# Which engine forms the low parts of the feed-forward weights: GpSimd before, VectorE after

## The chip, the cores and the metric

The kernel runs on one core of a Trainium2 chip. A core has five engines that each run their own instruction queue in order: TensorE (PE in the profile, with its weight loads as PEld), VectorE (DVE), ScalarE (ACT), GpSimd (POOL) and SyncE (SP), which here issues DMA transfers. The engines meet only at semaphores. The metric is device time in microseconds of one launch. Before the change three runs took 1326.4 to 1327.08 us, with a median of 1326.59.

## The reference

Two decoder layers on 512 tokens of width 1024 in fp32. Each layer is a mixer (gated linear attention and mLSTM in layer 0, stick-breaking and dilated attention in layer 1) and a SwiGLU feed-forward part, each with a modulation of its input and output that comes from a conditioning vector, and a normalization behind it. What the change touches is the feed-forward part, whose hidden width D_FF is 2816:

```
for layer in range(DEPTH):
    mod = c_act @ ada_w[layer] + ada_b[layer]            # six rows of 1024: shift, scale, gate, twice
    ...
    x = layer_norm(RES_ALPHA * x + (1.0 + g_m) * y, ln_g[layer, 0], ln_b[layer, 0])
    hf = x * (1.0 + sc_f) + sh_f
    yf = (jax.nn.silu(hf @ ffn_w1[layer]) * (hf @ ffn_w3[layer])) @ ffn_w2[layer]
    x = layer_norm(RES_ALPHA * x + (1.0 + g_f) * yf, ln_g[layer, 1], ln_b[layer, 1])
```

## The kernel before

**Split products.** TensorE multiplies fp32 operands as two parts. A weight tile arrives from HBM in `raw`; ScalarE writes its high part to `w_hi` (`to_hi`, L903), and another engine writes the low part, `w_lo = raw - w_hi`. The activations are split in the same way into `h_hi` and `h_lo`. A product is then three matmuls: weight high by activation low, high by high, and low by high (L1391 to L1393 in gate and up, L1441 to L1443 in down). A weight slot is 128 x 1024 values, 512 KB, and `raw`, `w_hi` and `w_lo` are rings of four slots each. Semaphores count the slots: `w_hi_ready`, `w_lo_ready`, and `slot_done` when TensorE has used one.

**Gate and up** (`ffn` on each engine). D_FF is cut into 11 steps of two 128-column blocks. A step uses four slots, two of gate and two of up, 96 matmuls. GpSimd forms the low parts of all of them (`split_range`, L832), one after another in a loop of four. VectorE's `step` (L2668) then does two things: `combine_weights` (L2660 to L2666) forms sums and differences of down-weight blocks, and L2677 to L2687 multiply gate by up into `hid` and form four sums of `hid`. Both kinds of sums serve the down product, which uses Strassen's scheme in Winograd's form: seven products of half-size blocks instead of eight. The down weights of a step are loaded into `combos` by DMAs that ScalarE issues, combined in place, and stored to a scratch area in HBM, 1 MB each way; ScalarE waits for `combo_step` before it issues the store.

**Modulation.** In layer 0 the loop of gate and up also computes the modulation rows of what follows. `two_steps` (L2710) runs two steps of the loop, and ahead of each it does four modulation products: `ada_acc` gets a 128 x 1024 tile of `ada_w` times one column of `c_act` added (L2717; L2720 for the first of eight). The tiles come through `ada_raw`, two buffers. Layer 1 has at most one smaller group of modulation products a step (`ada_block`), whose tiles are loaded apart.

**SyncE's loads.** In the loop of layer 0, SyncE issues in turn a weight load and a modulation load (L764 to L771):

```
for u in range(4):
    sp.wait_ge(sem("w_lo_ready"), 4 * j + (s0 + u - RAW + 1))
    sp.dma_start(raw[:, (s0 + u) % RAW, :], wstream[...])
    sp.wait_ge(sem("ada_step"), 4 * j + (36 + u - 1))
    sp.dma_start(ada_raw[:, u % 2, :], astream[...])
```

A weight load waits for the split four slots earlier, and a modulation load for the product that used its buffer; a waiting load holds back those behind it. The loads of iteration j begin at the stage's slot 4j, and its modulation waits count the products of step j. In layer 1 weight loads wait for the split four slots earlier alone.

**Down.** It has 42 slots, in the order P1, P5 and P6 in turn (18 slots), then P2, P3, P7 and P4 with six each; five pairs and a single one make the 11 steps. Some slots are 128 x 512, the rest 128 x 1024. Two slots of P4 (`HELD`) go to space that `hid_r` has left. GpSimd forms the low parts of the first four slots (`LO_FROM`) and from slot 30 on (`LO_TO`, L853 to L870), and VectorE those between (`down`, L2742, `lo`). Beside the weights, the factors of the products are split: ScalarE does the high parts (`a_hi`, `b1_hi`, `b2_hi`) and VectorE the low ones (`a_lo`, `b1_lo`, `b2_lo` at L2761 and L2762). In the last part, VectorE's and ScalarE's `b2` parts of step k stand behind the split of slot 21 + k.

**The end of down.** When P3's slots are used, the upper two token blocks are complete. VectorE's `norm` forms the residual and its statistics (`residual`, L2528 to L2546) and ScalarE normalizes (`normalizer`, L1133 to L1149), while TensorE works on P7 and P4, whose weights ScalarE still has to split. The place of `normalize(0)` among the `hi` calls of `down` is fixed in the code.

Of the kernel before, what the change touches and what calls it, by code (L numbers as in the profile page):

```python
# [17 lines left out]
ALU = mybir.AluOpType  # L18
# [21 lines left out]
RING = 4  # L40
# [68 lines left out]

DOWN = down_slots()  # L110
N_DOWN = len(DOWN)
LO_FROM, LO_TO = 4, 30
HELD = 38


# [115 lines left out]
def build_program(nc, wstream, astream, xT, vecs, const, const0, wa_up, dsel, rel, ln_rows, out):  # L231
# [595 lines left out]
    @block.gpsimd  # L827
    def _(pool):
        def split(s, slot):

            pool.wait_ge(sem("w_hi_ready"), s + 1)
            nc.gpsimd.tensor_tensor(w_lo[:, slot, :], raw[:, slot % RAW, :], w_hi[:, slot, :].bitcast(F32),  # L832
                                    ALU.subtract).then_inc(sem("w_lo_ready"), 1)

        assert RAW == RING

        def split_range(a, b):
            if b - a < 2 * RING:
                for s in range(a, b):
                    split(s, s % RING)  # L840
                return
            up, down = -(-a // RING) * RING, b // RING * RING
            for s in range(a, up):
                split(s, s % RING)
            with pool.Fori(up // RING, down // RING) as i:
                for u in range(RING):
                    split(RING * i + u, u)
            for s in range(down, b):
                split(s, s % RING)

        pool.wait_ge(sem("w_lo_ready"), len(FIRST))
        at_ = len(FIRST)
        for x in sorted(list(extra) + [DOWN0, DOWN1]):  # L853
            split_range(at_, x)
            at_ = x + 1
            if x in extra:
                pool.wait_ge(sem("w_hi_ready"), x + 1)
                nc.gpsimd.tensor_tensor(extra[x][1], raw[:, x % RAW, :], extra[x][0].bitcast(F32), ALU.subtract
                                        ).then_inc(sem("w_lo_ready"), 1)
                continue  # L860
            for s in range(x, x + LO_FROM):
                split(s, s % RING)
            pool.wait_ge(sem("w_lo_ready"), x + LO_TO)
            for m in range(LO_TO, N_DOWN):
                pool.wait_ge(sem("w_hi_ready"), x + m + 1)
                down_lo(nc.gpsimd, x, m).then_inc(sem("w_lo_ready"), 1)
            at_ = x + N_DOWN
        pool.wait_ge(sem("in_rows"), 16)
        for tb in range(1, TB - 1):
            pool.wait_ge(sem("xh_ready"), TB * 3 + tb + 1)  # L870
            nc.gpsimd.tensor_tensor(x_rows(tb), x_rows(tb), by_chunk(rows_gb[:, 0, :]), ALU.mult).then_inc(sem("scaled"), 1)
            pool.wait_ge(sem("scaled"), tb)
            nc.gpsimd.tensor_tensor(x_rows(tb), x_rows(tb), by_chunk(rows_gb[:, 1, :]), ALU.add).then_inc(sem("out_ready"), 1)
# [3 lines left out]
    def _(act):  # L877
# [41 lines left out]
        def warm_sqrt():  # L919

            nc.scalar.activation(warm[:], eps_col, ACT.Sqrt)
# [261 lines left out]
        def down(layer):  # L1183
# [4 lines left out]
            def hi(m):  # L1188
                to_hi(d + m, (d + m) % RING)
# [25 lines left out]
            for g in range(6):  # L1215
# [11 lines left out]
                    i.then_inc(sem("p1_copied"), 1)  # L1227
                hi(3 * g + 4)
                hi(3 * g + 5)
            for k in range(HALF_K):  # L1230
                hi(21 + k)
                b2_hi(k)
            hi(32)
            hi(33)
            warm_sqrt()
            normalize(0)
            hi(34)
            hi(35)
            normalize(1)
            for m in range(36, N_DOWN):  # L1240
                hi(m)
            done[0] = d + N_DOWN
            if layer == 1:
# [873 lines left out]
    def _(dve):  # L2117
# [528 lines left out]
        def ffn(layer, rest):  # L2646
# [18 lines left out]
                dve.wait_ge(sem("combo_step"), before + 3)  # L2665
                V.tensor_tensor(b21, b21, b11, ALU.subtract).then_inc(sem("combo_step"), 1)  # L2666

            def step(j, between=None):  # L2668

                combine_weights(j)  # L2670
                if between:
                    between()
                for b in range(2):
                    dve.wait_ge(*((sem("bank_full"), 2 * j + f0) if b == 0 else (sem("slot_done"), 4 * j + (s0 + 4))))
                    dve.wait_ge(sem("silu_ready"), 2 * j + (FC * layer + 1 + b))
                    split = lambda ap: ap.rearrange("q (o a x) -> q o a x", o=1, x=256)
                    V.tensor_tensor(block(j, (slice(0, 5, 4), slice(3, 7, 3))[b]), split(tmp[:, b, :]), split(ps[:, up + b, :]), ALU.mult  # L2677
                                    ).then_inc(sem("prod_ready"), 1)
                a11, s1, s2, a12, a21, s3, a22 = (block(j, a) for a in range(7))
                before = 4 * j + 4 * HALF_K * layer  # L2680
                dve.wait_ge(sem("prod_ready"), 2 * j + (FC * layer + 2))
                V.tensor_tensor(s1, a21, a22, ALU.add).then_inc(sem("s_step"), 1)
                V.tensor_tensor(s3, a11, a21, ALU.subtract).then_inc(sem("s_step"), 1)
                dve.wait_ge(sem("s_step"), before + 2)
                V.tensor_tensor(s2, s1, a11, ALU.subtract).then_inc(sem("s_step"), 1)  # L2685
                dve.wait_ge(sem("s_step"), before + 3)
                V.tensor_tensor(a21, a12, s2, ALU.subtract).then_inc(sem("s_step"), 1)  # L2687
# [21 lines left out]

            def two_steps(it, between=None):  # L2710

                for u in range(2):
                    for k in range(4 * u, 4 * u + 4):
                        dve.wait_ge(sem(f"ada_landed{k % 2}"), 64 * it + 16 * (12 + k // 2 + 1))
                        if k:
                            dve.wait_ge(sem("ada_step"), 8 * it + (40 + k))
                            V.scalar_tensor_tensor(ada_acc[:], ada_raw[:, k % 2, :], c_act[:, k:k + 1], ada_acc[:], ALU.mult,  # L2717
                                                   ALU.add).then_inc(sem("ada_step"), 1)
                        else:
                            V.tensor_scalar(ada_acc[:], ada_raw[:, 0, :], c_act[:, 0:1], None, ALU.mult  # L2720
                                            ).then_inc(sem("ada_step"), 1)
                    if u:
                        dve.wait_ge(sem("ada_step"), 8 * it + 48)
                        fold_rows()
                    step(2 * it + (u + 1), between if u else None)

            with dve.Fori(0, FC // 4 - 1) as it:
                two_steps(it)
# [12 lines left out]
        def down(layer):  # L2741
# [3 lines left out]
            def lo(m):  # L2745

                dve.wait_ge(sem("w_hi_ready"), d + m + 1)
                if m == LO_FROM:
                    dve.wait_ge(sem("w_lo_ready"), d + m)
                down_lo(V, d, m).then_inc(sem("w_lo_ready"), 1)  # L2750

            def b1_lo(k):
# [10 lines left out]
                                ALU.subtract).then_inc(sem("x_ready"), 1)  # L2763

            for g in range(6):
                if 3 * g + 3 >= LO_FROM:
                    lo(3 * g + 3)
                for k in (2 * g + 2, 2 * g + 3):
                    if k < HALF_K:
                        a_lo(layer, k)  # L2770
# [13 lines left out]
                        ins = V.tensor_tensor(u2_kept(r), p1_kept(r), by_half(ps[:, 5 + 2 * r, :]), ALU.add)  # L2784
                    ins.then_inc(sem("kept_added"), 1)
                lo(3 * g + 5)
            for k in range(HALF_K):
                if 21 + k < LO_TO:
                    lo(21 + k)
                b2_lo(k)  # L2790

        ffn(0, norm(0, "out0"))
        gate_col(1)
# [225 lines left out]
```

## Time and profile before

| | before |
|---|---|
| median of three runs | 1326.59 us (1326.4 to 1327.08) |
| the profiled execution | 1326.98 us, of which the span is 1325.2 |
| TensorE busy | 1254.8 us (95%) |
| TensorE weight loads busy | 1038.9 us (78%) |
| VectorE busy | 901.2 us (68%) |
| ScalarE busy | 528.5 us (40%) |
| GpSimd busy | 476.5 us (36%) |

The span is from the first to the last instruction of the profiled execution. Busy time is summed over instructions and says nothing of when they ran. The gate and up stage of layer 0 lies at about 319 to 547 us of the span, its down stage at 556 to about 665; layer 1's gate and up stage lies at about 965 to 1205 us and its down stage follows until the end. A timeline row begins with the start and the duration of an instruction or of a few equal ones in a row (xN), and ends with the idle time ahead of it on its engine and what ended that.

### The profile page before, as it was taken

The page shows a single profiled execution, that of the slowest core. Times are in us where ns is not written, and L with a number is a line of the kernel's source. Part 1 is how long each engine was busy: PE and PEld are TensorE (multiplying, and loading weights), DVE is VectorE, ACT ScalarE, POOL GpSimd, SP SyncE. Part 2 cuts the span into 40 slices and gives each one's busy share as a digit, 9 for nine tenths or more (in the row PEclk, how much of TensorE's full clock was granted, in tenths as well). Part 3 has the DMA queues.
Part 4 walks back from the last instruction along what each step waited for, and adds up shares of the span by engine and source line. Part 5 has one row for each costly group of instructions (what it writes and reads, how often), then busy time and mean ns, then how long its engine had stood idle before and what let it go on. Part 6 is the DMA issues. An engine that isn't in the chain of part 4 may idle for free.

```text
span 1325.2 us, 17193 instructions
## 1 busy us (share of the span) xinstructions
PE 1254.8 (95%) x6298; PEld 1038.9 (78%) x6298; DVE 901.2 (68%) x1244; ACT 528.5 (40%) x767; POOL 476.5 (36%) x195
## 2 busy tenths in 40 slices
PE   7999999998999999599899999999999999999996
PEld 6878887787787778488687777888888888888874
DVE  5489768868778777667766633358697636447785
ACT  3443364542212122366552455527342222225653
POOL 0243332423444444300645332222245444442046
PEclk9999999999999999799999999999999999999998
DMA  9981654534687777557446542212156665645843
GB/s 333 188 175 65 222 160 128 190 112 165 248 286 275 264 281 270 189 152 236 129 164 230 159 124 92 64 63 75 39 176 251 226 233 203 214 173 162 245 151 116
DMA packets 129362, 239.51 MB, mean 181 GB/s; under 512 B 18523, under 2 KB 83307, under 8 KB 126356
## 3 DMA queue, kind: packets, MB, share of 16 engines
q1 hardware_dynamic: 110792, 188.07, 45.5%
q10 hardware_dynamic: 18508, 50.62, 10.5%
q8 instruction: 38, 0.62, 0.2%
q14 instruction: 24, 0.20, 0.0%
HBM read 212.11 MB, written 27.59 MB: 181 GB/s over the span
## 4 chain that ended last, share of the span: by engine, by line
PE 60%; issue 17%; POOL 9%; DVE 8%; DMA 3%; ACT 1%; POOLq 0%; SPq 0%; DVEq 0%; ACTq 0%
PE ps L1391 10%; PE ps L1393 10%; PE ps L1392 10%; POOL w_lo L832 8%; PE ps L1441 4%; PE ps L1442 4%; PE ps L1443 4%; DMA ada_raw<-astream 2%; PE ps L1590 2%; PE ps L1591 2%; PE ps L1592 2%; PE ps L1556 1%; PE ps L1558 1%; PE ps L1557 1%; PE ps L1943 1%
## 5 line engine op out<-in xcount | busy, mean ns | idle before, releaser
L832 POOL TENSOR_TENSOR w_lo<-raw,w_hi 128x1024 fp32r<-128x1024 f32 x157 | 397.7, 2542 | 655.1 <-ACT w_hi L903 654.9
L903 ACT ACTIVATE w_hi<-raw 128x1024 fp32r<-128x1024 f32 (+1 forms) x235 | 238.9, 1031 | 498.2 <-DMA raw<-wstream 181.6
L1391 PE MATMUL ps<-h_lo,w_hi 128*128 128x512 f32 (+2 forms) x1064 | 399.5, 375 | 15.9 <-POOL w_lo L832 13.9
L1393 PE MATMUL ps<-h_hi,w_lo 128*128 128x512 f32 (+2 forms) x1064 | 394.6, 371 | 0.0
L1392 PE MATMUL ps<-h_hi,w_hi 128*128 128x512 f32 (+2 forms) x1064 | 394.6, 371 | 0.0
L1391 PEld LDWEIGHTS ps<-h_lo,w_hi 128*128 128x128 f32 (+1 forms) x1064 | 200.9, 189 | 57.3 <-issue 20.0
L1393 PEld LDWEIGHTS ps<-h_hi,w_lo 128*128 128x128 f32 (+1 forms) x1064 | 200.7, 189 | 34.8
L1392 PEld LDWEIGHTS ps<-h_hi,w_hi 128*128 128x128 f32 (+1 forms) x1064 | 200.9, 189 | 33.2
L650 POOL TENSOR_TENSOR w_lo<-raw,w_hi 128x1024 fp32r<-128x1024 f32 (+1 forms) x20 | 44.6, 2250 | 160.0 <-ACT w_hi L903 159.8
L2717 DVE SCALAR_TENSOR_TENSOR ada_acc<-ada_raw,c_act,ada_acc 128x1024 f32<-128x1024 f32 x35 | 58.8, 1679 | 45.1 <-DMA ada_raw<-astream 44.6
L2677 DVE TENSOR_TENSOR hid<-tmp,ps 128x512 f32<-128x512 f32 (+1 forms) x44 | 29.1, 683 | 86.2 <-PE ps L1393 86.2
L650 DVE TENSOR_TENSOR w_lo<-raw,w_hi 128x1024 fp32r<-128x1024 f32 (+1 forms) x52 | 57.6, 1121 | 30.8 <-ACT w_hi L903 30.4
L1441 PE MATMUL ps<-w_hi,hid_r 128*128 128x512 f32 x160 | 63.9, 400 | 8.2 <-issue 7.6
L2148 DVE SCALAR_TENSOR_TENSOR ada_acc<-ada_raw,c_act,ada_acc 128x1024 f32<-128x1024 f32 x35 | 60.8, 1737 | 12.0 <-DMA ada_raw<-astream 10.1
L1441 PE MATMUL ps<-w_hi,a_hl 128*128 128x512 f32 x132 | 52.5, 398 | 14.4 <-DVE mod L2154 14.4
L1442 PE MATMUL ps<-w_hi,hid_r 128*128 128x512 f32 x160 | 63.6, 398 | 0.0
L1443 PE MATMUL ps<-w_lo,hid_r 128*128 128x512 f32 x160 | 63.6, 398 | 0.0
L1442 PE MATMUL ps<-w_hi,a_hl 128*128 128x512 f32 x132 | 52.2, 395 | 0.0
L1443 PE MATMUL ps<-w_lo,a_hl 128*128 128x512 f32 x132 | 52.1, 394 | 0.0
L2685 DVE TENSOR_TENSOR hid<-hid 128x256 f32<-128x256 f32 (+1 forms) x22 | 48.1, 2186 | 1.6
L1441 PEld LDWEIGHTS ps<-w_hi,hid_r 128*128 128x128 f32 x160 | 30.8, 193 | 16.7 <-issue 9.3
L1590 PE MATMUL ps<-w_hi,h_lo 128*128 128x512 f32 (+1 forms) x112 | 41.8, 373 | 0.7 <-DVE kc L2807 0.7
(318 smaller groups left out, 2033.5 us busy)
## 6 DMA issues: line engine op xcount, KB each, us to landing
raw<-wstream SPq DMA_DIRECT2D x161, 512.0 KB, 4.5
ada_raw<-astream SPq DMA_DIRECT2D x80, 512.0 KB, 4.5
combos<-wstream ACTq DMA_DIRECT2D x22, 1024.0 KB, 5.5
combo_scratch<-combos ACTq DMA_DIRECT2D x22, 1024.0 KB, 3.9
raw<-combo_scratch SPq DMA_DIRECT2D x88, 256.0 KB, 3.3
raw<-wstream SPq DMA_DIRECT2D x66, 256.0 KB, 3.8
ada_first<-astream SPq DMA_DIRECT2D x16, 256.0 KB, 6.7
ada_first<-astream SPq DMA_DIRECT2D x8, 512.0 KB, 10.5
```

Source lines behind the costliest of these rows:

```text
L650: return engine.tensor_tensor(w_lo[:, s % RING, 0:n], raw[:, s % RAW, 0:n], w_hi[:, s % RING, 0:n].bitcast(F32), ALU.subtract)
L832: nc.gpsimd.tensor_tensor(w_lo[:, slot, :], raw[:, slot % RAW, :], w_hi[:, slot, :].bitcast(F32), ALU.subtract).then_inc(sem("w_lo_ready"), 1)
L903: nc.scalar.activation(w_hi[:, slot, 0:n], raw[:, slot, 0:n], ACT.Copy).then_inc(sem("w_hi_ready"), 1)
L1391: pe.matmul(o, w_h, x_l, start=start, stop=False)
L1392: pe.matmul(o, w_h, x_h, start=False, stop=False)
L1393: return pe.matmul(o, w_l, x_h, start=False, stop=stop)
L1441: pe.matmul(o, x_lo, w_h, start=begin, stop=False, skip_group_check=True)
L1442: pe.matmul(o, x_hi, w_h, start=False, stop=False, skip_group_check=True)
L1443: return pe.matmul(o, x_hi, w_l, start=False, stop=end, skip_group_check=True)
L1590: pe.matmul(o, h_lo[:, k, tokens], w_hi[:, s % RING, w], start=start, stop=False)
L2148: V.scalar_tensor_tensor(ada_acc[:], src, c_act[:, k:k + 1], ada_acc[:], ALU.mult, ALU.add).then_inc(sem("ada_step"), 1)
L2717: V.scalar_tensor_tensor(ada_acc[:], ada_raw[:, k % 2, :], c_act[:, k:k + 1], ada_acc[:], ALU.mult, ALU.add).then_inc(sem("ada_step"), 1)
```

## The change

VectorE takes over the low parts that GpSimd formed in both feed-forward stages: in gate and up all slots but the first four of a stage, in down the first thirty-two, so that GpSimd keeps the last ten, which belong to the products P7 (its last four) and P4. In layer 0, the four modulation products of a step are cut in two pairs, and the four splits too: two behind each pair. The slots that a step splits are the running step's fourth and the next step's first three. In down the `b2` parts come two steps at a time, so that they end by slot 26, and ScalarE does one more slot ahead of `normalize(0)`. TensorE's and SyncE's instructions are those of before.

```
-LO_FROM, LO_TO = 4, 30
+LO_TO = 32
...
-            split_range(at_, x)
+            split_range(at_, x if x in extra else SLOTS["ffn0" if x == DOWN0 else "ffn1"][0] + RING)
...
-            for s in range(x, x + LO_FROM):
-                split(s, s % RING)
...
-            for k in range(HALF_K):
-                hi(21 + k)
-                b2_hi(k)
-            hi(32)
-            hi(33)
+            for n in range(6):
+                hi(21 + n)
+                for k in (2 * n, 2 * n + 1):
+                    if k < HALF_K:
+                        b2_hi(k)
+            for m in range(27, 34):
+                hi(m)
             warm_sqrt()
+            hi(34)
             normalize(0)
-            hi(34)
             hi(35)
+            hi(36)
             normalize(1)
-            for m in range(36, N_DOWN):
+            for m in range(37, N_DOWN):
                 hi(m)
...
-            def step(j, between=None):
-
+            def step_lo(j, u):
+
+                slot = (s0 + u) % RING
+                dve.wait_ge(sem("w_hi_ready"), 4 * j + (s0 + u + 1))
+                V.tensor_tensor(w_lo[:, slot, :], raw[:, slot, :], w_hi[:, slot, :].bitcast(F32), ALU.subtract
+                                ).then_inc(sem("w_lo_ready"), 1)
+
+            def step(j, between=None, beside=None):
+
+                if beside:
+                    beside(0)
+                if not isinstance(j, int) or j:
+                    step_lo(j, 3)
+                else:
+                    dve.wait_ge(sem("w_lo_ready"), s0 + RING)
+                step_lo(j, 4)
                 combine_weights(j)
+                if beside:
+                    beside(1)
+                step_lo(j, 5)
+                step_lo(j, 6)
                 if between:
                     between()
...
-                for u in range(2):
-                    for k in range(4 * u, 4 * u + 4):
+                def ada(u, part):
+
+                    for k in range(4 * u + 2 * part, 4 * u + 2 * part + 2):
...
-                    if u:
+                    if u and part:
                         dve.wait_ge(sem("ada_step"), 8 * it + 48)
                         fold_rows()
-                    step(2 * it + (u + 1), between if u else None)
+
+                for u in range(2):
+                    step(2 * it + (u + 1), between if u else None, lambda part: ada(u, part))
...
             def lo(m):
 
                 dve.wait_ge(sem("w_hi_ready"), d + m + 1)
-                if m == LO_FROM:
-                    dve.wait_ge(sem("w_lo_ready"), d + m)
                 down_lo(V, d, m).then_inc(sem("w_lo_ready"), 1)
...
             for g in range(6):
-                if 3 * g + 3 >= LO_FROM:
-                    lo(3 * g + 3)
+                lo(3 * g + 3)
...
-            for k in range(HALF_K):
-                if 21 + k < LO_TO:
-                    lo(21 + k)
-                b2_lo(k)
+            for n in range(6):
+                lo(21 + n)
+                for k in (2 * n, 2 * n + 1):
+                    if k < HALF_K:
+                        b2_lo(k)
+            for m in range(27, LO_TO):
+                lo(m)
```

The first place is VectorE's program at the head of the first two steps inside layer 0's loop. Before, it reads so (ISA and REGISTER_ALU rows are waits and the counts for them; `combos` rows are `combine_weights`):

```order
L2720 TENSOR_SCALAR ada_acc<-ada_raw,c_act 128x1024
L2716 ISA
L2717 SCALAR_TENSOR_TENSOR ada_acc<-ada_raw,c_act,ada_acc 128x1024
L2714 REGISTER_ALU
L2716 REGISTER_ALU
L2717 SCALAR_TENSOR_TENSOR ada_acc<-ada_raw,c_act,ada_acc 128x1024
L2716 REGISTER_ALU
L2717 SCALAR_TENSOR_TENSOR ada_acc<-ada_raw,c_act,ada_acc 128x1024
L2659 ISA
L2660 TENSOR_TENSOR combos<-combos 128x2x256
L2661 ISA
L2662 TENSOR_TENSOR combos<-combos 128x2x256
```

The same place of VectorE's program after the change, up to the combination:

```order
L2740 TENSOR_SCALAR ada_acc<-ada_raw,c_act 128x1024
L2736 ISA
L2737 SCALAR_TENSOR_TENSOR ada_acc<-ada_raw,c_act,ada_acc 128x1024
L2672 ISA
L2673 TENSOR_TENSOR w_lo<-raw,w_hi 128x1024
L2672 REGISTER_ALU
L2673 TENSOR_TENSOR w_lo<-raw,w_hi 128x1024
L2660 ISA
L2661 TENSOR_TENSOR combos<-combos 128x2x256
```

And from the end of the combination on, ahead of the gate by up product:

```order
L2667 TENSOR_TENSOR combos<-combos 128x2x256
L2734 REGISTER_ALU
L2736 REGISTER_ALU
L2737 SCALAR_TENSOR_TENSOR ada_acc<-ada_raw,c_act,ada_acc 128x1024
L2736 REGISTER_ALU
L2737 SCALAR_TENSOR_TENSOR ada_acc<-ada_raw,c_act,ada_acc 128x1024
L2672 REGISTER_ALU
L2673 TENSOR_TENSOR w_lo<-raw,w_hi 128x1024
L2672 REGISTER_ALU
L2673 TENSOR_TENSOR w_lo<-raw,w_hi 128x1024
```

The four modulation products stood together ahead of the combination; now two stand ahead of it and two behind it, and each pair is followed by two splits that wait for ScalarE's high parts.

The second place is ScalarE's program at the end of layer 0's down stage, around `normalize(0)` (`cols`, `nmr` and `xa` rows). Before:

```order
L903 ACTIVATE w_hi<-raw 128x1024
L1209 ACTIVATE hid_r<-hid 128x256
L1210 ACTIVATE hid_r<-hid 128x256
L903 ACTIVATE w_hi<-raw 128x1024 x2
L921 ACT_TABLE_LOAD
L921 ACTIVATE warm<-vec_eps 128x1
L1133 ACTIVATE cols<-mv,vec_eps 128x1
L1134 ACTIVATE cols<-mv 128x1
L1146 ACTIVATE nmr<-cols,cst,rstd 128x1
L1149 ACTIVATE xa<-xa,nmr,rstd 128x8x128
L903 ACTIVATE w_hi<-raw 128x1024
L903 ACTIVATE w_hi<-raw 128x512
```

The same place after the change:

```order
L901 ACTIVATE w_hi<-raw 128x512
L901 ACTIVATE w_hi<-raw 128x1024 x4
L919 ACT_TABLE_LOAD
L919 ACTIVATE warm<-vec_eps 128x1
L901 ACTIVATE w_hi<-raw 128x1024
L1131 ACTIVATE cols<-mv,vec_eps 128x1
L1132 ACTIVATE cols<-mv 128x1
L1144 ACTIVATE nmr<-cols,cst,rstd 128x1
L1147 ACTIVATE xa<-xa,nmr,rstd 128x8x128
L901 ACTIVATE w_hi<-raw 128x512
L901 ACTIVATE w_hi<-raw 128x1024
```

One weight slot more is ahead of the wait for the statistics, and the `b2` parts (`hid_r<-hid`) have moved forward.

The third place is VectorE's program at the end of the same stage, ahead of the residual (`ps` rows; `scl` rows derive the next modulation). Before:

```order
L650 TENSOR_TENSOR w_lo<-raw,w_hi 128x512
L2761 TENSOR_TENSOR hid_r<-hid,hid_r 128x256
L2762 TENSOR_TENSOR hid_r<-hid,hid_r 128x256
L2761 TENSOR_TENSOR hid_r<-hid,hid_r 128x256
L2762 TENSOR_TENSOR hid_r<-hid,hid_r 128x256
L2761 TENSOR_TENSOR hid_r<-hid,hid_r 128x256
L2762 TENSOR_TENSOR hid_r<-hid,hid_r 128x256
L2182 SCALAR_TENSOR_TENSOR scl<-mod,vec 128x8
```

After the change:

```order
L2781 TENSOR_TENSOR hid_r<-hid,hid_r 128x256
L2782 TENSOR_TENSOR hid_r<-hid,hid_r 128x256
L650 TENSOR_TENSOR w_lo<-raw,w_hi 128x1024 x2
L650 TENSOR_TENSOR w_lo<-raw,w_hi 128x512
L650 TENSOR_TENSOR w_lo<-raw,w_hi 128x1024 x2
L2183 SCALAR_TENSOR_TENSOR scl<-mod,vec 128x8
```

The last `b2` parts stood directly ahead of the residual; now five weight splits stand there.

## Rows read from the trace of the kernel before

**Rows 1.** The page: busy time of each engine; costliest groups, and by shape.

```profile
PE 1254.8 (95%) x6298; PEld 1038.9 (78%) x6298; DVE 901.2 (68%) x1244; ACT 528.5 (40%) x767; POOL 476.5 (36%) x195
...
L832 POOL TENSOR_TENSOR w_lo<-raw,w_hi 128x1024 fp32r<-128x1024 f32 x157 | 397.7, 2542 | 655.1 <-ACT w_hi L903 654.9
...
L650 DVE TENSOR_TENSOR w_lo<-raw,w_hi 128x1024 fp32r<-128x1024 f32 x42 | 51.0, 1224 | 28.8 <-ACT w_hi L903 28.4
```

**Rows 2.** Windows: length, busy of PE, PEld, DVE, ACT, POOL, granted clock, DMA share, GB/s.

```profile
328.30:332.20 3.90, 3.90 (x9) 3.08 (x10) 3.87 (x3) 1.74 (x3) 2.88 (x1) 0.50 0.85 307
376.00:398.00 22.00, 21.69 (x96) 17.64 (x94) 17.04 (x15) 4.78 (x6) 9.77 (x4) 1.00 0.77 270
556.40:560.90 4.50, 4.50 (x11) 3.53 (x12) 2.81 (x4) 0.00 (x0) 0.00 (x0) 0.50 0.00 0
649.70:653.10 3.40, 3.40 (x10) 2.66 (x9) 0.00 (x0) 3.24 (x4) 1.78 (x2) 0.50 0.74 233
970.00:1202.00 232.00, 232.00 (x1088) 194.20 (x1086) 133.56 (x136) 63.01 (x73) 109.23 (x43) 1.00 0.59 211
1291.40:1294.80 3.40, 3.40 (x10) 2.63 (x9) 2.63 (x2) 3.40 (x4) 1.79 (x2) 0.50 0.86 273
```

**Rows 3.** Timeline of VectorE over one step of layer 0's loop.

```profile
358.94 1.28 DVE L2677 TENSOR_TENSOR hid<-tmp,ps 128x512 f32 x2
360.49 0.43 DVE L2682 TENSOR_TENSOR hid<-hid  x1 [0.27 <-DVE hid L2677]
...
363.82 2.51 DVE L2687 TENSOR_TENSOR hid<-hid  x1
...
366.32 0.74 DVE L2720 TENSOR_SCALAR ada_acc<-ada_raw,c_act 128x1024 f32<-128x1024 f32 x1
...
370.42 1.28 DVE L2717 SCALAR_TENSOR_TENSOR ada_acc<-ada_raw,c_act,ada_acc 128x1024 f32<-128x1024 f32 x1 [2.03 <-DMA ada_raw<-astream]
...
376.54 0.68 DVE L2660 TENSOR_TENSOR combos<-combos 128x512 f32<-128x512 f32 x1
```

**Rows 4.** Timeline of SyncE's DMA queue in the same step.

```profile
367.09 0.33 SPq L770 DMA_DIRECT2D ada_raw<-astream  x1
367.62 0.33 SPq L767 DMA_DIRECT2D raw<-wstream  x1
...
369.29 0.33 SPq L767 DMA_DIRECT2D raw<-wstream  x1
```

**Rows 5.** Timeline of ScalarE in the same step.

```profile
372.00 1.06 ACT L903 ACTIVATE w_hi<-raw 128x1024 fp32r<-128x1024 f32 x1 [10.27 <-DMA raw<-wstream]
375.67 1.06 ACT L903 ACTIVATE w_hi<-raw 128x1024 fp32r<-128x1024 f32 x1 [2.61 <-DMA raw<-wstream]
```

**Rows 6.** VectorE's first modulation product of step 1 and of step 10.

```profile
318.93 0.75 DVE L2720 TENSOR_SCALAR ada_acc<-ada_raw,c_act 128x1024 f32<-128x1024 f32 x1
...
526.12 2.66 DVE L2717 SCALAR_TENSOR_TENSOR ada_acc<-ada_raw,c_act,ada_acc 128x1024 f32<-128x1024 f32 x2
```

**Rows 7.** TensorE's waits in layer 0: step 1, one later step, down's start.

```profile
328.27 0.77 PE L1391 MATMUL ps<-h_lo,w_hi 128*128 128x512 f32 x1 [5.67 <-POOL w_lo L832]
...
398.52 0.47 PE L1391 MATMUL ps<-h_lo,w_hi 128*128 128x512 f32 x1 [0.83 <-POOL w_lo L832]
...
556.38 0.77 PE L1441 MATMUL ps<-w_hi,a_hl 128*128 128x512 f32 x1 [14.22 <-DVE mod L2154]
```

**Rows 8.** The end of down: layer 0 (VectorE, ScalarE, TensorE), then layer 1.

```profile
633.65 2.62 DVE L2762 TENSOR_TENSOR hid_r<-hid,hid_r 128x256 fp32r<-128x256 f32 x1
...
643.68 0.30 ACT L1133 ACTIVATE cols<-mv,vec_eps 128x1 f32<-128x1 f32 x1 [7.33 <-DVE mv L2539]
...
645.77 1.56 ACT L903 ACTIVATE w_hi<-raw 128x1024 fp32r<-128x1024 f32 x2
...
649.33 0.47 PE L1441 MATMUL ps<-w_hi,hid_r 128*128 128x512 f32 x1 [4.79 <-issue]
...
1290.58 0.47 PE L1441 MATMUL ps<-w_hi,hid_r 128*128 128x512 f32 x1 [2.12 <-issue]
```

## The prediction

> **What bounds the kernel now.** I read the page first, then the windows by stage, then one step of the first layer's gate and up loop engine by engine, then the waits around its end and around the end of both down stages. The page shows TensorE busy 95% of the span and VectorE 68% [rows 1]; the shares hide that stages differ. In the windows the second layer's loop has TensorE busy 232.00 of 232.00 us, while a quiet stretch of the first layer's loop takes 22.0 us for one step of 96 matmuls [rows 2]. So in the second layer nothing but the matmuls sets the pace, and splits moved there can gain nothing.
>
> In the first layer a step is longer than its matmuls. The first modulation product of step 1 ends at 318.93 + 0.75 = 319.68 and that of step 10 at 526.12 + 1.28 = 527.40 [rows 6]: nine steps take 207.7 us, 23.1 each, 1.1 more than the matmuls. The missing time is TensorE waiting for a split: 5.67 us in step 1, then about a microsecond a step (0.83 in the row shown), and 14.22 us before the down stage [rows 7]. What it waits for can be followed in one step. VectorE ends its first modulation product at 366.32 + 0.74 = 367.06 [rows 3]; SyncE, which was waiting for exactly that, issues the next modulation load at 367.09 and only behind it, at 367.62, the weight load of the fourth slot of the running step; the next weight load goes out at 369.29, after the second product [rows 4]. ScalarE starts on the two weights at 372.00 and 375.67 [rows 5]. The weight stream of this layer is thus paced by VectorE's modulation products, two products per two slots. Before the change VectorE does all four products before anything else of the step, and no VectorE instruction waits for a weight; GpSimd does.
>
> **The change part by part.** Per layer 46 splits go from GpSimd (2542 ns each) to VectorE (1224 ns) [rows 1]: 40 of gate and up, the first four of down, and down's 31st and 32nd. GpSimd's 110 us were beside other work; VectorE's 56 us a layer stand in an in-order queue, and that is what has to be priced.
>
> First layer, gate and up. VectorE's step becomes: products 1 and 2, split of the fourth slot, split of the next step's first, combination of down weights, products 3 and 4, splits of the next step's second and third, gate times up, four sums. SyncE's program is unchanged. So the two weights whose splits stand right behind products 1 and 2 are those that SyncE issues after products 1 and 2, and the same again with 3 and 4: VectorE now sits through the landing of each pair, twice a step, and queued behind the waiting split are the combination, the other products, and with them the next weight loads. I call L the time from the end of an odd product to the moment ScalarE can start on the pair's second weight. From below: issued 2.23 us after the product (369.29 - 367.06), landing as fast as the weight that had one transfer ahead of it, 372.00 - 367.62 = 4.38: L = 6.6. From above, as that row has it: 375.67 - 367.06 = 8.6 [rows 4, 5]. I take 7.5, the middle: the same four loads in the same order, but without the next four on their heels, and in the second pair with a 1 MB store beside them. The serial rest of a step: high part 1.06 and split 1.22 with hand-offs, 2.5, twice, 5.0; combination 4 x 0.68 with gaps 2.9; product 3, 1.3; gate times up 1.3; four sums of 0.43, 1.75; modulation and next product 1 (0.74 or 1.28) 1.1 [rows 1, 3, 5]. Together 13.35, so a step is 13.35 + 2L: 28.4 us, with 26.6 and 30.6 as ends. Against 23.1 that is +5.3 a step (+3.5 to +7.5), over the nine steps +47.7 (+31.5 to +67.5).
>
> What is taken off in that loop: the sums and combinations no longer wait for GpSimd; the last sum took 2.51 us against 0.43 for one that did not wait [rows 3]. That relief is already in the terms above. At the loop's start I count -1 (between -2 and 0: two waits on GpSimd go, three splits come). Behind the last step 556.38 - 527.40 = 29.0 us pass before down's first matmul [rows 6, 7]; the combined weights are now stored while products 3, 4 and the splits run instead of ahead of the split pairs, but the pair's wait is added: -2.5 (between -5 and 0).
>
> The Trainium skill, page "SBUF — State Buffer", section "Who interferes with whom", says that a VectorE instruction with two SBUF inputs and a GpSimd instruction that reads SBUF exclude each other for a whole instruction; the 2.51 us row agrees. By that rule alone every step would lose about 4 us of waiting and none would be added: the second rival's mechanism. Against the change speaks the page "DMA: Bandwidth & Descriptors", section "Anatomy of one DMA": a semaphore wait happens on the issuing sequencer, before a transfer is dispatched. The 0.03 us between product and issue agree. By it a weight behind a waiting load is not even under way, and the pair's landing comes on top.
>
> TensorE in this loop: two waits of 2 to 3 us a step. The trace shows it at 0.50 of its clock (1.2 of 2.4 GHz) for some microseconds after its waits of 5.67, 14.22, 4.79 and 2.12 us [rows 2, 7, 8]. One stretch of 3.4 us costs 1.7; two a step make 22.0 + 3.4 = 25.4, still under 28.4, so I cost it at nothing; without that cover it would be the first rival.
>
> Second layer, gate and up: 0. Its weight loads wait only for the split four slots earlier, so each is under way a step ahead; VectorE's 133.56 us of 232 [rows 2] plus 49 for 40 splits leaves room. From below 0, since TensorE never waits there; from above +10, a microsecond a step.
>
> Down, both layers. Before, VectorE's last pair splits run against GpSimd's (2.62 us for one subtraction, as long as the sum of 2.51 [rows 3, 8]), so the first residual and ScalarE's normalization are late. ScalarE waits 7.33 us for them with the next weight behind it in its queue, starts on that at 645.77, and TensorE stands 4.79 us [rows 8], then runs 3.4 us at half clock [rows 2], 1.7 more. After the change the pair splits end by slot 26, VectorE does slots 30 and 31 itself, and ScalarE takes the 35th slot before it waits: I expect the stall gone, -6.5. The second layer's is 2.12 and again 1.7 [rows 2, 8]: -3.8. Together -10.3, between -11 and 0. New in this part: two pair splits per slot, 1.22 + 2 x 0.86 = 2.9 us of VectorE for 2.7 of TensorE over six slots, covered by the slots already split.
>
> Sum: 47.7 - 1 - 2.5 - 10.3 = +34. The profiled execution took 1326.98 (span 1325.2 and 1.8 around it), 0.4 above the median of the runs: 1361 against it, 1360 as a median. Ends: 31.5 - 7 - 11 = +13, 1340; 67.5 and no relief but down's, 1384.
>
> **The rivals.** First, the half clock: if the two waits a step kept TensorE at 1.2 GHz throughout, 96 matmuls would take about 43 us instead of 22, and nine steps 180 more: 1500. For it: every wait above 2 us in the rows was followed by a half-clock stretch. Against: full clock came back within 4 to 5 us of work each time. Second, the other side: the waits for landings are covered and only the relief counts. Then the loop falls to TensorE's 22.0 (9 x 1.1 = 10), step 1's 5.67 goes, and down gives 10: 1301. It decides where 13.35 + 2L reaches 23.1, L = 4.9; for it the 2.51 us rows, against it that the pair's second load is issued 2.2 us in and a transfer with one ahead of it already needs 4.4. Third, the down stages stay as they are, because the residual or the last splits on GpSimd find another wait: +44, 1371. Fourth, the pair lands much nearer to its issue than any row (L 5 to 6): 1327 to 1340.
>
> **How the numbers follow.** Forecast 0.70; half clock 0.05; other side 0.09; no gain in down 0.12; fourth 0.04, of which three parts in four too small to tell. 0.2% is about what a measurement of this kernel can tell from no change. Slower 0.70 + 0.05 + 0.12 + 0.01 = 0.88, same 0.03, faster 0.09. The range leaves out the half clock, the other side and the fourth, and is the forecast's own: 1338 to 1384.
>
> **What would show it.** Right: in the first layer's loop VectorE idle twice a step with ScalarE's high part as releaser, some 4 us each, steps of 26.6 to 30.6 us, TensorE waiting twice a step for VectorE's split; the second layer's loop still without a TensorE wait; no wait of 4.79 and 2.12 late in down. Wrong: first-layer steps of 22 us, waits for a weight in the second layer, or those late waits still there.

## The result and the profile after

The changed kernel takes 1378.94 us (median of four runs, 1378.49 to 1382.55) against 1326.84 before: ratio 1.0399, 95% interval 1.0381 to 1.0417. The forecast was 1360 with 1338 to 1384 as its range; direction and mechanism held, and a loss of 34 us was forecast where 52 came. The profiled execution took 1379.32 us with a span of 1377.4, 52.2 more than before.

The page after the change, first the busy times, then the group of VectorE's new splits (busy us, mean ns of one, idle time ahead of it and what ended that):

```profile
PE 1269.4 (92%) x6298; PEld 1049.3 (76%) x6298; DVE 873.1 (63%) x1336; ACT 529.3 (38%) x767; POOL 243.6 (18%) x103
...
L2673 DVE TENSOR_TENSOR w_lo<-raw,w_hi 128x1024 fp32r<-128x1024 f32 x86 | 104.7, 1223 | 211.5 <-ACT w_hi L901 211.5
```

VectorE took over 105 us of splits in gate and up and yet is busy 28 us less than before [rows 1], since its other instructions no longer meet GpSimd's: the sum of `hid` that took 2.51 us in [rows 3] takes 0.42 after the change. But it now stands 211.5 us ahead of these splits, waiting for ScalarE's high part. Where that happens is told by the first modulation product of step 1 and of step 10 (as [rows 6]):

```profile
318.28 0.75 DVE L2740 TENSOR_SCALAR ada_acc<-ada_raw,c_act 128x1024 f32<-128x1024 f32 x1
...
595.00 2.66 DVE L2737 SCALAR_TENSOR_TENSOR ada_acc<-ada_raw,c_act,ada_acc 128x1024 f32<-128x1024 f32 x2
```

Nine steps take 596.28 - 319.03 = 277.25 us, 30.8 each instead of 23.1: +69.5 us. The chain of waits over one step shows what a step is made of (start, us, what):

```profile
443.54 1.29 DVE ada_acc L2737
444.85 0.33 SPq L770
...
445.73 6.03 DMA raw<-wstream
451.86 1.07 ACT w_hi L901
...
454.10 0.69 DVE combos L2661
...
456.88 1.29 DVE ada_acc L2737
458.33 0.33 SPq L770
...
458.85 1.04 SPq L767
459.98 1.14 SPq L770
461.32 6.08 DMA raw<-wstream
467.42 1.07 ACT w_hi L901
...
469.65 1.29 DVE hid L2696 x2
...
472.90 1.29 DVE ada_acc L2737
```

TensorE is not in it at all. Twice a step the chain goes from a product to SyncE, from there into a weight load of 6 us, to ScalarE and back to VectorE. In the windows (columns as in [rows 2]: the last 1.9 us of the wait in step 2 with the half-clock stretch behind it, the step above, layer 1's loop) TensorE is busy 25.05 of 30.8 us in layer 0's step, at half clock for a part of it, and 232.00 of 232.00 us in layer 1:

```profile
342.00:348.60 6.60, 4.69 (x11) 3.76 (x12) 4.41 (x6) 1.56 (x2) 0.00 (x0) 0.50 0.55 205
...
443.50:474.30 30.80, 25.05 (x96) 19.82 (x95) 15.43 (x20) 5.20 (x6) 0.00 (x0) 0.89 0.57 204
...
1027.00:1259.00 232.00, 232.00 (x1087) 194.29 (x1087) 137.33 (x182) 63.01 (x73) 0.00 (x0) 1.00 0.59 212
```

TensorE's waits in step 1, in step 2 and, in two pieces around eight small matmuls of the modulation, ahead of down, which answer to [rows 7]; then ScalarE ahead of the normalization in down (7.33 us of idle in [rows 8]):

```profile
326.22 0.47 PE L1392 MATMUL ps<-h_lo,w_hi 128*128 128x512 f32 x1 [2.97 <-DVE w_lo L2673]
...
343.91 0.77 PE L1392 MATMUL ps<-h_lo,w_hi 128*128 128x512 f32 x1 [6.56 <-DVE w_lo L2673]
...
614.78 0.30 PE L1605 MATMUL ps<-ada_part,cst 128*32 128x8 f32 x8 [5.33 <-DVE ada_part L2159]
...
621.95 0.76 PE L1442 MATMUL ps<-w_hi,a_hl 128*128 128x512 f32 x1 [6.86 <-DVE mod L2155]
```

```profile
702.79 0.29 ACT L1131 ACTIVATE cols<-mv,vec_eps 128x1 f32<-128x1 f32 x1 [0.40 <-DVE mv L2540]
```

ScalarE waits 0.40 us there, and between 690 and 724 us no TensorE row shows a wait. From the start of the first to the start of the last matmul layer 0's down takes 107.9 us (116.1 before, from 556.38 to 672.5 us of the span, where the section on time and profile has about 665) and layer 1's 105.0 (110.1). So the 52 us are +69.5 in layer 0's loop, -13.4 in the two down stages, and -4 at the loop's two ends.

### The profile page after: what moved, and what is told of

It is laid out like the page before. It is cut to its first block, busy times and chain, and to the rows that moved or that the text cites. A ratio compares the mean times of both kernels' runs of the same rounds, so it can differ in the third digit from the quotient of the medians.

```text
span 1377.4 us, 17095 instructions
## 1 busy us (share of the span) xinstructions
PE 1269.4 (92%) x6298; PEld 1049.3 (76%) x6298; DVE 873.1 (63%) x1336; ACT 529.3 (38%) x767; POOL 243.6 (18%) x103
## 4 chain that ended last, share of the span: by engine, by line
PE 60%; DVE 16%; DMA 10%; issue 6%; ACT 3%; SPq 2%; POOL 2%; DVEq 0%; POOLq 0%; ACTq 0%
PE ps L1392 9%; PE ps L1393 9%; PE ps L1394 9%; DMA raw<-wstream 8%; PE ps L1442 4%; PE ps L1444 4%; PE ps L1443 4%; DVE ada_acc L2737 3%; ACT w_hi L901 2%; PE ps L1591 2%; PE ps L1844 2%; PE ps L1846 2%; PE ps L1845 2%; PE ps L1593 2%; PE ps L1592 2%
## 5 line engine op out<-in xcount | busy, mean ns | idle before, releaser
L1392 PE MATMUL ps<-h_lo,w_hi 128*128 128x512 f32 (+2 forms) x1064 | 407.7, 383 | 48.6 <-DVE w_lo L2673 43.0
L1393 PE MATMUL ps<-h_hi,w_hi 128*128 128x512 f32 (+2 forms) x1064 | 402.1, 378 | 0.0
L1394 PE MATMUL ps<-h_hi,w_lo 128*128 128x512 f32 (+2 forms) x1064 | 401.4, 377 | 0.0
L832 POOL TENSOR_TENSOR w_lo<-raw,w_hi 128x1024 fp32r<-128x1024 f32 x69 | 174.6, 2539 | 364.2 <-ACT w_hi L901 364.1
L2673 DVE TENSOR_TENSOR w_lo<-raw,w_hi 128x1024 fp32r<-128x1024 f32 x86 | 104.7, 1223 | 211.5 <-ACT w_hi L901 211.5
L1393 PEld LDWEIGHTS ps<-h_hi,w_hi 128*128 128x128 f32 (+1 forms) x1064 | 205.5, 193 | 34.5
L650 POOL TENSOR_TENSOR w_lo<-raw,w_hi 128x1024 fp32r<-128x1024 f32 (+1 forms) x16 | 33.8, 2137 | 735.5 <-ACT w_hi L901 735.5
L650 DVE TENSOR_TENSOR w_lo<-raw,w_hi 128x1024 fp32r<-128x1024 f32 (+1 forms) x58 | 65.0, 1128 | 34.4 <-ACT w_hi L901 33.7
L2149 DVE SCALAR_TENSOR_TENSOR ada_acc<-ada_raw,c_act,ada_acc 128x1024 f32<-128x1024 f32 x35 | 61.2, 1749 | 11.8 <-DMA ada_raw<-astream 9.7
L1442 PE MATMUL ps<-w_hi,a_hl 128*128 128x512 f32 x132 | 52.2, 395 | 6.9 <-DVE mod L2155 6.9
L2737 DVE SCALAR_TENSOR_TENSOR ada_acc<-ada_raw,c_act,ada_acc 128x1024 f32<-128x1024 f32 x35 | 44.9, 1281 | 1.3 <-DVE ada_acc L2740 0.5
L1593 PE MATMUL ps<-w_lo,h_hi 128*128 128x512 f32 (+1 forms) x112 | 40.4, 361 | 0.0
```

What stands on the lines that cost most here:

```text
L650: return engine.tensor_tensor(w_lo[:, s % RING, 0:n], raw[:, s % RAW, 0:n], w_hi[:, s % RING, 0:n].bitcast(F32), ALU.subtract)
L1392: pe.matmul(o, w_h, x_l, start=start, stop=False)
L1393: pe.matmul(o, w_h, x_h, start=False, stop=False)
L1394: return pe.matmul(o, w_l, x_h, start=False, stop=stop)
L1442: pe.matmul(o, x_lo, w_h, start=begin, stop=False, skip_group_check=True)
L2673: V.tensor_tensor(w_lo[:, slot, :], raw[:, slot, :], w_hi[:, slot, :].bitcast(F32), ALU.subtract).then_inc(sem("w_lo_ready"), 1)
```

## The experiments

The theory under test: VectorE sits through the landing of weights that SyncE issues only behind VectorE's own modulation products, and a step is a serial rest plus the two waits L. Each ratio is against the kernel before, run beside that experiment, whose median was 1327.82, 1327.61 or 1328.25 us; differences between two experiments are of their medians.

**Weight loads three slots earlier in SyncE's program.**

```
-        for s in range(s0, s0 + 4):
+        AHEAD = 3
+        for s in range(s0, s0 + 4 + AHEAD):
             load(s)
-        with sp.Fori(1, FC // 2) as j:
+        with sp.Fori(1, FC // 2 - 1) as j:
             for u in range(4):
-                sp.wait_ge(sem("w_lo_ready"), 4 * j + (s0 + u - RAW + 1))
+                w = s0 + u + AHEAD
+                sp.wait_ge(sem("w_lo_ready"), 4 * j + (w - RAW + 1))
...
+        for u in range(4):
+            if u < 4 - AHEAD:
+                load(s0 + 4 * (FC // 2 - 1) + u + AHEAD)
+            load_ada(4 * (FC // 2 - 1) + 36 + u)
```

> The changed kernel, with one thing moved: in SyncE's loop of layer 0 each weight load is issued three slots earlier among the modulation loads, so that the weights that VectorE splits in a step are under way before that step's modulation products. Theory (VectorE sits through the landing of weights that are issued only behind its own products): the two waits a step go, a step falls from 30.8 us to TensorE's 22 to 23, nine steps give back 70 to 79 us: 1300 to 1309. Rival 1 (the 49 us of splits in VectorE's in-order queue are themselves the cost): VectorE's work in a step is what it was, the time stays above 1360. Rival 2 (the transfers are slow because loads and the 1 MB stores share the DMA engines, wherever they are issued): steps of 26 to 29 us, 1335 to 1362.

1290.62 us, ratio 0.9712 (0.9696 to 0.9728): 88 us less than the change alone, and 37 less than before. The window over layer 0's loop, and TensorE's wait ahead of down:

```profile
320.00:526.00 206.00, 206.00 (x935) 169.45 (x933) 149.75 (x180) 50.58 (x56) 0.00 (x0) 1.00 0.81 293
```

```profile
533.36 0.77 PE L1448 MATMUL ps<-w_hi,a_hl 128*128 128x512 f32 x1 [6.91 <-DVE mod L2161]
```

TensorE is busy for the whole 206 us at full clock. VectorE does exactly the work of the changed kernel, so the work is not the cost (rival 1), and the same loads and stores run beside them (rival 2). It went below the range that I gave: the steps run at 22 us, as expected, and the waits in steps 1 and 2, which I had not counted apart, went too.

**Small modulation loads.**

```
-   sp.dma_start(ada_raw[:, u % 2, :], astream[... (36 + u)])
+   sp.dma_start(ada_raw[:, u % 2, 0:P], astream[... (36 + u), :, 0:P])
```

> The changed kernel, with the modulation loads of layer 0's loop cut from 512 KB to 64 KB each (the modulation rows computed there are then not the reference's); every wait and the order of the loads stay. It splits the wait for a pair of weights in two: waiting to be issued, and sharing the DMA engines with the modulation tiles. Theory: the second weight of a pair still goes out 2.2 to 3.2 us after the odd product but lands in about 4.4 us instead of 6, so the wait L falls from 8.8 to about 7, a step from 30.8 to about 27, and the time by about 33, to 1346 (1338 to 1355). If the landing is all latency and no sharing: unchanged, 1379. If sharing is all of it: L near 4.5, a step at TensorE's 22 to 23, 1300 to 1310.

1343.88 us, ratio 1.0121 (1.0103 to 1.0139), as expected. ScalarE's high parts of one first pair (the odd product ended at 451.93):

```profile
455.99 1.06 ACT L901 ACTIVATE w_hi<-raw 128x1024 fp32r<-128x1024 f32 x1 [9.77 <-DMA raw<-wstream]
458.62 1.06 ACT L901 ACTIVATE w_hi<-raw 128x1024 fp32r<-128x1024 f32 x1 [1.57 <-DMA raw<-wstream]
```

L is 6.7 here; over nine steps 6.6 in the first pair and 7.3 in the second, where the changed kernel has 8.2 and 9.75. From its issue to ScalarE's start the second weight of a pair takes 4.3 and 4.4 us here, 5.9 and 6.6 in the changed kernel. So 1.6 us of the first wait and 2.4 of the second go with the modulation tiles that land beside the weights; the rest is the late issue and the landing itself.

**The store later.**

```
-                combos_out(layer, j)
+                if layer:
+                    combos_out(layer, j)
                 for s in (5, 6):
...
+                if not layer:
+                    combos_out(layer, j)
```

> The changed kernel, with ScalarE's store of the combined down weights of layer 0 (1 MB) issued behind the high parts of the step's last two weights instead of ahead of them. In the trace two of SyncE's issues in the second pair of a step take 1.05 and 1.1 us instead of 0.33, in nine steps of nine, 1.2 us after that store was issued. Theory (the store beside them causes this): the long issues go, the second pair's L falls from 9.4 by 1.5, and with less sharing perhaps by 2.5; nine steps give 13 to 23 us: 1356 to 1366. Rival (the issues are slow for another reason, as what SyncE does there): they stay at 1.05 to 1.1 us and the time stays within 4 us of 1379, or the store meets the next loads and gives back what was won.

1372.51 us, ratio 1.0333 (1.0316 to 1.035): 6.4 us, half of the least that I expected. SyncE's two issues in a second pair, and ScalarE behind them:

```profile
453.41 0.33 SPq L767 DMA_DIRECT2D raw<-wstream  x1
454.06 0.33 SPq L770 DMA_DIRECT2D ada_raw<-astream  x1
```

```profile
461.30 1.06 ACT L901 ACTIVATE w_hi<-raw 128x1024 fp32r<-128x1024 f32 x1 [2.55 <-DMA raw<-wstream]
```

The long issues are gone in all nine steps (18 of them before), so the store's place made them. Without them the second weight of the pair goes out 1.9 us behind the odd product instead of 3.1, but it still needs 6.6 us from its issue (6.7 for the one issued at 454.58): L went from 9.75 to 8.5 in the second pair. In the first it rose from 8.2 to 8.7, so 0.5 us of the 1.25 won went back. The store and the next combination load now lie closer to that pair's loads, which would do it; that was not tried apart.

In all three kernels that still wait, the step is the two L and 12.9 us more: 8.2 + 9.75 + 12.9 = 30.8, 6.6 + 7.3 + 12.9 = 26.8, 8.7 + 8.5 + 12.9 = 30.1, against 30.8, 26.8 and 30.05 measured. Nothing is left over for TensorE's clock.

**Layer 0's gate and up back on GpSimd.**

```
-            split_range(at_, x if x in extra else SLOTS["ffn0" if x == DOWN0 else "ffn1"][0] + RING)
+            split_range(at_, SLOTS["ffn1"][0] + RING if x == DOWN1 else x + 3 if x == DOWN0 else x)
...
                 if beside:
                     beside(0)
+                    beside(1)
...
-                step_lo(j, 4)
+                if layer:
...
+                    step_lo(j, 4)
                 combine_weights(j)
-                if beside:
-                    beside(1)
-                step_lo(j, 5)
-                step_lo(j, 6)
+                if layer:
+                    step_lo(j, 5)
+                    step_lo(j, 6)
```

> The changed kernel, with one part undone: in layer 0's gate and up GpSimd forms the low parts again (and those of down's first three slots), and VectorE does its four modulation products together as before; layer 1's gate and up and both down stages stay as changed. Theory (all the loss is in layer 0's loop, and the down stages gained 8.3 and 5.1 us): 1326.8 - 13.4 = 1313, 1310 to 1317. Rival (the gains in the down stages come from GpSimd's absence ahead of them, or layer 1's loop lost something that the down stage hides): 1319 to 1330.

1312.65 us, ratio 0.9882 (0.9865 to 0.9899). The change is worth 15 us without this one part, and the whole loss is in it.

**The same SyncE order in the kernel before.** The edit of the first experiment, in the kernel before.

> The kernel before, with SyncE's weight loads of layer 0's loop issued three slots earlier among the modulation loads; GpSimd forms the low parts as before. Theory (the 1.1 us a step that TensorE lost before the change came from the same place in SyncE's queue, only that GpSimd waited for the landing and not VectorE): a step of 23.1 falls to about 22.1 and the wait of 5.67 us in step 1 goes for the most part, 1326.8 - 9 - 5 = 1313, 1309 to 1318. Rival (TensorE waited for GpSimd because a split takes it 2.5 us): within 3 us of 1326.8.

1322.65 us, ratio 0.9961 (0.9943 to 0.9978): 5 us less, where I expected 14.

```profile
340.10 0.77 PE L1397 MATMUL ps<-h_lo,w_hi 128*128 128x512 f32 x1 [6.28 <-POOL w_lo L838]
...
552.11 0.77 PE L1447 MATMUL ps<-w_hi,a_hl 128*128 128x512 f32 x1 [13.97 <-DVE mod L2160]
```

The waits inside the loop went but for 0.9 us and less (a step 22.4 us), as the theory has it, but not those at its ends: an early wait of 6.28 us behind GpSimd (5.67 before), and 13.97 us ahead of down.

**The same with down and layer 1 as changed.** The edits of the first and of the fourth experiment together.

> The run with layer 0's gate and up splits back on GpSimd (1312.7), now with the weight loads three slots earlier as in the run with loads ahead (1290.6). It asks what VectorE's splits in that loop are worth once no engine waits for a landing. Theory (nothing, TensorE sets the pace with either engine): 1291, up to 1295. Rival (GpSimd's instructions hold up VectorE's sums, or its slower split shows at the loop's ends): 1298 to 1304.

1308.84 us, ratio 0.986 (0.9837 to 0.9883): my theory fell. With the loads early, layer 0 takes 18 us more with GpSimd's splits and the four products together than with VectorE's splits and the products in pairs. What the place of the splits does can be read ahead of step 1, in VectorE's row for the same line of the normalization in this run, then in the run with loads ahead:

```profile
314.18 3.42 DVE L2611 TENSOR_TENSOR xa<-xa,ln_rows 128x1024 f32<-128x1024 f32 x1
```

```profile
313.26 1.22 DVE L2611 TENSOR_TENSOR xa<-xa,ln_rows 128x1024 f32<-128x1024 f32 x1
```

While GpSimd splits, VectorE's instruction takes 3.42 us instead of 1.22. The Trainium skill, page "SBUF — State Buffer", section "Who interferes with whom", has a VectorE instruction with two SBUF inputs contend with a GpSimd instruction that reads SBUF, under an exclusive lock; these rows agree. The first modulation product is 5.2 us later for it, and with it the modulation and weight loads; TensorE then waits 6.51 us early in the loop and 12.79 ahead of down, where the run with loads ahead has 0 and 6.91. How the 18 us divide between these hold-ups and VectorE's shorter split was not tried; what the pairs have to do with it is asked below.

**Down's new order alone, in the kernel before.** (`LO_TO` 32, the `b2` parts two steps at a time, ScalarE's slot 34 ahead of `normalize(0)`; the diff is the one shown for `down`.)

> The kernel before, with the down stages' new order alone: the b2 parts two steps at a time, VectorE's splits up to slot 32 instead of 30, one slot more on ScalarE ahead of the first normalization; GpSimd keeps gate and up of both layers and down's first four slots. Theory (the 13.4 us that the down stages won come from this order): 1326.8 - 13.4 = 1313, 1312 to 1317. Rival (they need GpSimd out of the way of gate and up or of down's first slots): 1319 to 1327.

1314.84 us, ratio 0.9908 (0.9881 to 0.9934), its down stages 108.1 and 105.1 us long against 107.9 and 105.0 in the changed kernel: the whole gain of down comes from its order.

**Weight loads one slot earlier.** The first edit with 1 in place of 3.

> The changed kernel with the weight loads of layer 0's loop issued one slot earlier, not three. Of a pair the first weight is then issued ahead of the step's odd product and the second right behind it, 0.55 us after its end. Theory (the wait L is counted from that product to the second landing): L near 5.0 in the first pair and 6.1 to 6.8 in the second, a step of 13.2 + 5 + 6.4 = 24.6, nine steps 56 us less than 1379: 1322, 1314 to 1336. Rival (what counts is only whether a step's loads are out before the step): still 29 to 31 us a step, 1362 to 1379; or all gone with the first slot: 1290 to 1300.

1325.23 us, ratio 0.9977 (0.9964 to 0.999). ScalarE's high part of the second weight in a first and in a second pair (the odd products ended at 443.86 and 455.13):

```profile
448.83 1.06 ACT L907 ACTIVATE w_hi<-raw 128x1024 fp32r<-128x1024 f32 x1 [6.84 <-DMA raw<-wstream]
...
461.76 1.06 ACT L907 ACTIVATE w_hi<-raw 128x1024 fp32r<-128x1024 f32 x1 [6.06 <-DMA raw<-wstream]
```

L is 5.0 and 6.6 here, 5.35 and 6.6 over nine steps; with 12.9 that is 24.85 a step, and 24.84 was measured. So the time falls by degrees as the loads go out earlier, and not all at once.

**The four products together again, with loads ahead.**

```
                 if beside:
                     beside(0)
+                    beside(1)
...
-                if beside:
-                    beside(1)
```

> The run with loads ahead (1290.6), but VectorE does the four modulation products of a step together ahead of the first split, as it did before the change. With the splits on GpSimd and the loads ahead the time was 1308.8; this asks how much of those 18 us comes from cutting the products in two pairs. Theory (the pairs matter only behind the last step, where the combination and its store then come later): TensorE's wait ahead of down grows from 6.9 us to 10 to 13, 1290.6 + 5 = 1296, 1293 to 1299. Rival (the pairs also keep TensorE fed in the loop, since products 3 and 4 wait for tiles that are issued after products 1 and 2): waits in every step, 1300 to 1325. If the pairs are worth nothing: 1290 to 1292.

1317.54 us, ratio 0.9919 (0.9903 to 0.9936): the rival held. VectorE at the third and fourth product of a step:

```profile
446.37 1.29 DVE L2742 SCALAR_TENSOR_TENSOR ada_acc<-ada_raw,c_act,ada_acc 128x1024 f32<-128x1024 f32 x1 [4.39 <-DMA ada_raw<-astream]
448.90 1.28 DVE L2742 SCALAR_TENSOR_TENSOR ada_acc<-ada_raw,c_act,ada_acc 128x1024 f32<-128x1024 f32 x1 [1.24 <-DMA ada_raw<-astream]
```

It now sits through the landing of modulation tiles, which are issued behind products 1 and 2, with the splits queued behind it; a step is 24.2 us. With the products cut in pairs, two splits and the combination fill that time. So the pairs were needed, and 27 of the 37 us hang on them. Without them VectorE's splits are 9 us slower than GpSimd's (1308.84): the 18 us above come from the splits and the pairs together. GpSimd's splits with the products in pairs were not tried.

**The combination one split earlier, with loads ahead.**

```
-                step_lo(j, 4)
+                if layer:
+                    step_lo(j, 4)
                 combine_weights(j)
+                if not layer:
+                    step_lo(j, 4)
```

> The run with loads ahead (1290.6), with the combination of layer 0's down weights one split earlier in a step, between the splits of the fourth slot and of the next step's first. In the last step that second split is of down's first slot and waits some 8 us for its weight; the combination, its store and all behind it wait with it, and TensorE stands 6.9 us ahead of down. Theory: the combination and the store go 3 to 8 us earlier, the wait falls to 3 to 5 us: 1287.5, 1285 to 1290. Rival (the wait ahead of down is set by the last gate by up product and the modulation behind it): unchanged within 1.5 us.

1288.95 us, ratio 0.9695 (0.9675 to 0.9715): within the range given, though 1.7 us under the run with loads ahead is little against runs of 1285.04 to 1289.55. The wait that the edit aimed at did shrink, 3.76 us where 6.91 stood:

```profile
530.42 0.47 PE L1448 MATMUL ps<-w_hi,a_hl 128*128 128x512 f32 x1 [3.76 <-DVE mod L2161]
```

Its median is the lowest, 3% below the kernel before; whether it beats the run with loads ahead is open, since the intervals of the two ratios overlap.

## Why the prediction was right, and where its size was off

- **First layer's loop: right mechanism, wrong size.** The forecast was a step of 13.35 + 2L with L = 7.5, 28.4 us; measured were 12.9 us and waits of 8.2 and 9.75, 30.8. The serial rest was 0.45 too long; the term that was mis-sized is L, taken at 7.5, near the middle of 6.6 and 8.6 (which is 7.6), and short by 2.9 us over the two pairs. That is 2.4 a step, 22 us over nine. The upper end, the one that a row showed in full, was nearer: over nine steps ScalarE starts on the second weight 5.9 us after its issue in the first pair and 6.6 in the second, near the 375.67 - 369.29 = 6.4 of [rows 4, 5] and not the 4.4 of the first weight, and in the second pair two issues of about 1.1 us came on top, which [rows 4] do not have. The expected easing (no next four loads on their heels) was 0.5 us in the first pair and none in the second. The sign "some 4 us each" for VectorE's idle time was too small as well: in the step shown it is 4.91 and 1.99 us in one pair, 6.44 and 1.37 in the other.
- **Loop's start and end:** -1 and -2.5 forecast, -0.65 and -3.3 measured.
- **Half clock cost nothing in the loop:** waits of up to 6.56 us were followed by stretches at 0.50 of the clock, and the step is still its two waits and the serial rest. The first rival failed: the clock over a whole step was 0.89 and not 0.50.
- **Second layer's loop: 0 forecast, -0.4 measured**, TensorE busy throughout.
- **Down: -10.3 forecast, -13.4 measured.** The waits of 4.79 and 2.12 and the half-clock stretches behind them went, by the order alone, as the run with down's order shows. The rest I did not count: small waits near the end of both stages in the kernel before went or shrank (0.59 us to none, 0.71 to 0.21), and layer 0's first matmuls run at half clock for 3.1 us, now behind the waits of 5.33 and 6.86, where it was 4.5 us behind the one of 14.22. The third rival, no gain in down, failed.

```profile
664.05 0.47 PE L1441 MATMUL ps<-w_hi,hid_r 128*128 128x512 f32 x1 [0.59 <-ACT w_hi L903]
...
1305.88 0.47 PE L1441 MATMUL ps<-w_hi,hid_r 128*128 128x512 f32 x1 [0.71 <-issue]
```

- **The other side:** its condition, landings that are covered, did not hold in the changed kernel, but the run with loads ahead made it hold, and came to 1290.6, below the 1301 of that rival, which had left out the wait ahead of down (14.22 us before, 6.91 there) and taken 10 for the down stages.
- **Two figures that do not add up:** the fourth rival, L of 5 to 6, gives by the forecast's own terms steps of 23.35 to 25.35 us and a time of 1315 to 1333, not 1327 to 1340; it failed with L at 8.2 and 9.75. And 46 splits of 2542 ns are 117 us of GpSimd, not 110. The forecast rests on neither.

## What to carry to other kernels

When an in-order engine takes over work from one that only waited, follow back what the new work waits for: if its input is issued behind an instruction of the same engine, the engine waits for itself, for the whole landing, and the landing is longer for the transfers beside it. The cure is in the issuing queue, which has to move together with the work: the same change lost 52 us or won 37 by the place of the weight loads in SyncE's program. Price such a wait by the longest landing that the trace shows in company, not by a middle.

## What was not expected of the hardware

In the changed kernel two of SyncE's issues in the second pair of a step took 0.99 to 1.15 us instead of 0.33, in nine steps of nine (18 issues). In the step shown ScalarE's queue had issued the 1 MB store of the combined weights at 457.12; the load issued 1.2 us after that took 0.33, the two issued 1.7 and 2.9 us after it 1.04 and 1.14. With the store moved, all took 0.33. The same long issues appear with modulation loads of 64 KB, 0.88 to 1.05 us. What in the issue waits is not shown by the trace.
